# A decoder step in fp32 on one Trainium2 core: the last w_down group with tokens in PSUM's partitions, and reordered ScalarE and VectorE queues

## What is computed

```
def sq_relu_mlp(x, w_up, w_down):
    return jnp.square(jax.nn.relu(x @ w_up)) @ w_down

x = layer_norm(ALPHA * x + h, ln_g[layer, 0], ln_b[layer, 0])
x = layer_norm(ALPHA * x + sq_relu_mlp(x, w_up[layer], w_down[layer]), ln_g[layer, 1], ln_b[layer, 1])
```

## Time and profile before

| | us |
|---|---|
| median of 3 runs (lowest, highest) | 945.35 (944.09, 947.1) |
| the profiled execution, its own time | 946.36 |
| its span in the profile | 944.5 |
| PE busy | 919.8 (97%) |
| DVE busy | 629.2 (67%) |
| ACT busy | 430.9 (46%) |
| POOL busy | 56.3 (6%) |
| mean granted TensorE clock | 0.991 |

### The profile page before, as it was taken

One profiled execution on the slowest core, in us unless ns is written; L12 is line 12 of the kernel. 1 busy time (PEld: TensorE's weight loads), 2 busy tenths in 40 slices (PEclk: granted clock), 3 DMA queues, 4 the chain that ended last, 5 costly groups with the idle time before them and its releaser, 6 DMA issues.

```text
span 944.5 us, 18995 instructions
## 1 busy us (share of the span) xinstructions
PE 919.8 (97%) x7618; PEld 855.7 (91%) x7618; DVE 629.2 (67%) x1116; ACT 430.9 (46%) x801; POOL 56.3 (6%) x69
## 2 busy tenths in 40 slices
PE   9999989999999999999999999998999999999996
PEld 8999877899999999998887778877899999999994
DVE  6576568768877575676576747454468797757555
ACT  5344654356445263445344453343347644536321
POOL 0000005400000000320000000000120000000000
PEclk9999999999999999999999999999999999999997
DMA  9962213754454544566887997999855545544301
GB/s 289 279 204 90 90 45 90 214 155 139 139 169 139 173 136 143 175 211 223 290 299 241 330 368 295 392 373 340 271 175 152 160 149 185 158 134 154 115 1 56
DMA packets 134224, 182.79 MB, mean 194 GB/s; under 512 B 5845, under 2 KB 116125, under 8 KB 134136
## 3 DMA queue, kind: packets, MB, share of 16 engines
q1 hardware_dynamic: 128750, 177.29, 57.2%
q10 hardware_dynamic: 4746, 2.18, 0.9%
q0 software_dynamic: 640, 2.10, 0.8%
HBM read 175.23 MB, written 6.32 MB: 192 GB/s over the span
## 4 chain that ended last, share of the span: by engine, by line
PE 91%; DVE 4%; DMA 2%; ACT 1%; issue 1%; SPq 0%; ACTq 0%; DVEq 0%; POOL 0%; POOLq 0%
PE ps L550 24%; PE ps L552 23%; PE ps L551 23%; PE ps L887 6%; PE ps L929 3%; PE ps L985 2%; DMA page<-in_cache_v_dram 2%; PE ps L565 1%; PE ps L583 1%; PE ps L736 0%; PE ps L970 0%; PE ps L649 0%; DVE gate_o L1543 0%; DVE w_lo L1457 0%; PE ps L567 0%
## 5 line engine op out<-in xcount | busy, mean ns | idle before, releaser
L1085 ACT ACTIVATE w_hi<-raw 128x1024 fp32r<-128x1024 f32 x192 | 202.6, 1057 | 257.6 <-PE ps L552 248.4
L1457 DVE TENSOR_TENSOR w_lo<-raw,w_hi 128x1024 fp32r<-128x1024 f32 x192 | 235.1, 1225 | 113.0 <-ACT w_hi L1085 112.7
L550 PE MATMUL ps<-x_hi,w_hi 128*128 128x322 f32 (+1 forms) x888 | 279.4, 315 | 1.3 <-ACT k_turned L1355 1.3
L552 PE MATMUL ps<-x_hi,w_lo 128*128 128x322 f32 (+1 forms) x888 | 276.3, 311 | 0.0
L551 PE MATMUL ps<-x_lo,w_hi 128*128 128x322 f32 (+1 forms) x888 | 275.9, 311 | 0.0
L550 PE MATMUL ps<-h_hi,w_hi 128*128 128x320 f32 x632 | 197.4, 312 | 1.7 <-DVE h_lo L1595 1.7
L552 PE MATMUL ps<-h_hi,w_lo 128*128 128x320 f32 x632 | 195.8, 310 | 0.0
L551 PE MATMUL ps<-h_lo,w_hi 128*128 128x320 f32 x632 | 195.7, 310 | 0.0
L550 PEld LDWEIGHTS ps<-x_hi,w_hi 128*128 128x128 f32 x888 | 168.0, 189 | 6.5 <-ACT k_turned L1355 4.2
L551 PEld LDWEIGHTS ps<-x_lo,w_hi 128*128 128x128 f32 x888 | 168.5, 190 | 0.2
L552 PEld LDWEIGHTS ps<-x_hi,w_lo 128*128 128x128 f32 x888 | 167.5, 189 | 0.0
(11 more groups left out here) (349 smaller groups left out, 908.7 us busy)
## 6 DMA issues: line engine op xcount, KB each, us to landing
raw<-in_w_up_dram SPq DMA_DIRECT2D x32, 1024.0 KB, 5.7
raw<-in_w_down_dram SPq DMA_DIRECT2D x32, 1024.0 KB, 5.1
page<-in_cache_k_dram SPq DMA_DIRECT2D x64, 512.0 KB, 5.5
page<-in_cache_v_dram SPq DMA_DIRECT2D x64, 512.0 KB, 6.4
raw<-in_w_in_a_dram SPq DMA_DIRECT2D x12, 1024.0 KB, 9.2
raw<-in_w_kv_dram SPq DMA_DIRECT2D x8, 1024.0 KB, 6.8
raw<-in_w_out_a_dram SPq DMA_DIRECT2D x4, 1024.0 KB, 5.1
raw<-in_w_q_b_dram SPq DMA_DIRECT2D x4, 1024.0 KB, 5.3
```

Of the source, the lines that this page charges most:

```text
L550: mm(out, WH[t % SPL][:, k, :], hi[:, k, 0:width], start=(k == 0), stop=False)
L552: last = mm(out, WL[t % SPL][:, k, :], hi[:, k, 0:width], start=False, stop=(k == 7))
L1085: A(WH[t % SPL][:, :, :], raw[RBUF[u]][:, :, 128 * (t % 2):128 * (t % 2) + 128], ACT.Copy)\
L1457: V.tensor_tensor(WL[t % SPL][:, :, :], raw[RBUF[t // 2]][:, :, 128 * (t % 2):128 * (t % 2) + 128], WH[t % SPL][:, :, :].bitcast(F32), ALU ...
```

## The change

**The last quad.** Its 1024 rows of w_down are now loaded as rows with all 1024 columns: tile k is 128 rows (hidden columns of chunk k) by 1024. The roles are swapped: the hidden activations are stationary, 128 tokens at a time, and the weights move, 512 columns in one product, so the result has tokens in PSUM's partitions: banks 2 to 5 for two prompt tiles by two halves, banks 0 and 1 for the sample. The sample's hidden parts lie side by side in `HS` (64 columns hi, 64 lo), so that one product with `WH` makes hi in the partitions 0 to 63 and lo in 64 to 127, and one with `WL` only needs 64 columns. The stream x is added to the same banks by products of x (stationary) with the identity (`x_turn`). The last four tiles are all kept: the sample is finished first, then each prompt tile and half in turn.

**The end.** The statistics are taken from 512 columns at once (`y_stats`), each token tile is finished when its banks are complete; ACT copies the sample's lo part out of the upper partitions, DVE adds it, ACT scales the sample, POOL adds its bias, and SP stores it ahead of the prompt. The gain-and-bias pair, the sample's detour through PE and the joined statistics are gone.

**The queues.** `decay(h + 1)` is made ahead of `weights(h)`; `v_copy(7)` stands ahead of `normalised(6)`; `gated(7)` and `h_rest(7)` ahead of `state(0)`; the masked v is made by ACT (`masked`) instead of POOL; the two products of the prompt's n sum go to different columns of the array and DVE adds them; in `p_step` ACT copies what PE made ahead of the next exponent, and DVE's `head_low` stands ahead of `p_norm`.

The diff, cut to its core:

```diff
@@ -366,6 +361,17 @@
                 return ps[n % 2]
             return ps[(0, 1, 6, 7)[t % 4]]
 
+        def summed(i, half):
+
+
+            return ps[(2, 4, 0)[i] + half][:, :]
+
+        def raw_tile(t):
+            r = raw[RBUF[t // 2]]
+            if t // 8 == Q_LAST:
+                return r[:, 4 * (t % 2):4 * (t % 2) + 4, :].rearrange("p k (a n) -> p (k a) n", a=2)
+            return r[:, :, 128 * (t % 2):128 * (t % 2) + 128]
+
         def x_bank(n):
 
             return ps[(2, 3, 4, 6, 7, 1)[n % 6]]
...
@@ -424,6 +430,9 @@
                     kind, g = MLP_ORDER[q - first]
                     if kind == "u":
                         return lhs_k(w_up[m][:, 1024 * g + c:1024 * g + c + 256])
+                    if q == Q_LAST:
+                        rows = w_down[m][1024 * g + c:1024 * g + c + 256, :]
+                        return rows.rearrange("(a p) (k n) -> p a k n", p=128, k=4)
                     return lhs_k(w_down[m][1024 * g:1024 * g + 1024, c:c + 256])
             w, c0 = {Q_QK: (win, 0), Q_V: (win, 1024), Q_O: (win, 2048), Q_WOA: (w_out_a[0], 0),
                      Q_WK: (w_kv, 0), Q_WV: (w_kv, 1024), Q_WQ: (w_q_b[0], 0), Q_WOB: (w_out_b[0], 0)}[q]
...
+            sp.dma_start(y_sample.rearrange("b t c -> (b t) c"), Yt[0:64, 2, :]).then_inc(s_yp, 16)
             sp.wait_ge(s_yf, 1)
             sp.dma_start(y_prompt[0, 0:128, :], Yt[:, 0, :]).then_inc(s_yp, 16)
...
@@ -726,7 +739,7 @@
                     j = n - 2
                     pe.wait_ge(s_wk, 8)
                     pe.wait_ge(s_hg, H)
-                    pe.wait_ge(s_vm, 2 * j + 2)
+                    pe.wait_ge(s_vm, j + 1)
                     for half in range(2):
                         if j >= 2:
                             pe.wait_ge(s_cadd, 2 * j - 3 + half)
...
                         mm(o, wsK[:, q, 64 * h:64 * h + 64], VT[:, q, h, 0:128],
                            start=(q == 0), stop=(q == 1), skip_group_check=True)
-                for q in range(2):
-                    mm(ps[5][0:1, :], ones[:, 0:1], wsK[:, q, :], start=(q == 0), stop=(q == 1))
-                mm(ps[5][32:40, :], bmask[0:64, :], wsK[0:64, 2, :], start=True, stop=True).then_inc(s_np, 1)
+                mm(ps[5][0:1, :], ones[:, 0:1], wsK[:, 0, :], start=True, stop=True, skip_group_check=True)
+                mm(ps[5][64:65, :], ones[:, 0:1], wsK[:, 1, :], start=True, stop=True, skip_group_check=True)
+                mm(ps[5][32:40, :], bmask[0:64, :], wsK[0:64, 2, :], start=True, stop=True, skip_group_check=True)\
+                    .then_inc(s_np, 1)
 
             def ln_stats(l):
 
...
+            def x_turn(n):
+
+                pe.wait_ge(*emptied(8 * (Q_LAST - 1) + n))
+                c = slice(128 * (n % 4), 128 * (n % 4) + 128)
+                for i in range(3):
+                    tok = slice(128 * i, min(128 * i + 128, T))
+                    mm(summed(i, n // 4)[0:tok.stop - tok.start, c], X[:, n, tok], ident, start=False, stop=False,
+                       skip_group_check=True)
+
+            def flat(w, half):
+                return w[:, :, :].rearrange("p k n -> p (k n)")[:, 512 * half:512 * half + 512]
+
+            def down_prompt(k, i, half):
+
+                t, out, tok = 8 * Q_LAST + k, summed(i, half), slice(128 * i, 128 * i + 128)
+                wh, wl = flat(WH[t % SPL], half), flat(WL[t % SPL], half)
+                mm(out, HH[1][:, k, tok], wh, start=(k == 0), stop=False, skip_group_check=True)
+                mm(out, HH[1][:, k, tok], wl, start=False, stop=False, skip_group_check=True)
+                return mm(out, HL[1][:, k, tok], wh, start=False, stop=(k == 7), skip_group_check=True)
+
+            def down_sample(k):
+
+
+                t = 8 * Q_LAST + k
                 for half in range(2):
-                    mm(ps[4 + half][0:64, :], msT[:, :], gb2[:, 512 * half:512 * half + 512], start=False, stop=True,
-                       skip_group_check=True).then_inc(s_yz, 1)
+                    mm(summed(2, half), HS[:, k, :], flat(WH[t % SPL], half), start=(k == 0), stop=(k == 7),
+                       skip_group_check=True)
+                    last = mm(summed(2, half)[0:64, :], HS[:, k, 0:64], flat(WL[t % SPL], half), start=False,
+                              stop=(k == 7), skip_group_check=True)
+                return last
+
+            def last_down():
+                t = 8 * Q_LAST
+                pe.wait_ge(s_hl, 40 + 8 * 3 + 8)
+                pe.wait_ge(s_evr, 2)
+                for k in range(4):
+                    pe.wait_ge(s_lo, t + k + 1)
+                    for i in range(2):
+                        for half in range(2):
+                            down_prompt(k, i, half)
+                    if k == 0:
+                        pe.wait_ge(*emptied(t - 3))
+                    down_sample(k).then_inc(s_mm, 1)
+                    for n in ((), (0, 1, 2), (3, 4), (5, 6))[k]:
+                        x_turn(n)
+                for k in (4, 5, 6):
+                    pe.wait_ge(s_lo, t + k + 1)
+                    down_sample(k)
+                x_turn(7)
+                pe.wait_ge(s_lo, t + 8)
+                down_sample(7).then_inc(s_acc, 1)
+                for i in range(2):
+                    for half in range(2):
+                        for k in (4, 5, 6, 7):
+                            last = down_prompt(k, i, half)
+                        last.then_inc(s_acc, 1)
 
             def mlp(l, q0, hl0):
                 for i, (kind, g) in enumerate(MLP_ORDER):
...
@@ -1193,8 +1233,8 @@
                     normalised(h - 2)
                 if h >= 3:
                     h_rounded(h - 3)
+            v_copy(7)
             normalised(6)
-            v_copy(7)
             h_rounded(5)
             normalised(7)
             h_rounded(6)
@@ -1208,6 +1248,16 @@
             def gain_bias(l):
                 A(XH[:, :, T:TW], lnrow(lnT, l), ACT.Copy).then_inc(s_gbh, 1)
 
+            def masked(j):
+
+                if j == 0:
+                    act.wait_ge(s_hg, H)
+                    act.wait_ge(s_vc, 8)
+                for b in range(4):
+                    ins = A(Vm[:, 2 * j:2 * j + 2, b, :], VT[0:64, 2, 2 * j:2 * j + 2, 0:128], ACT.Copy,
+                            scale=bmask4[0:64, b:b + 1])
+                ins.then_inc(s_vm, 1)
+
             def x_rounded(l, n):
 
                 act.wait_ge(s_xr, 8 * l + n + 1)
...
                             if 8 * g + n >= 2:
                                 act.wait_ge(s_hl, hl0 + 8 * g + n - 1)
                             A(FS[n % 2][:, :], f[:, :], ACT.Square)
-                            A(HH[g % 2][:, n, :], f[:, :], ACT.Square).then_inc(s_hh, 1)
+                            if l == 2 and g == 3:
+                                A(HH[g % 2][:, n, 0:TP], f[:, 0:TP], ACT.Square)
+                                A(HS[:, n, 0:TS], f[:, TP:T], ACT.Square).then_inc(s_hh, 1)
+                            else:
...
@@ -1329,13 +1382,13 @@
                 A(PTt[h % 2][:, :], ps[3][:, 0:384], ACT.Copy).then_inc(s_pTc, 1)
 
             def p_step(i):
-                if 0 <= i < H:
-                    p_exp(i)
                 if 0 <= i - 2 < H:
                     act.wait_ge(s_pV, i - 2 + 1)
                     A(HH[0][:, i - 2, 0:TP], ps[0][:, 0:256], ACT.Copy).then_inc(s_xhp, 1)
                 if 0 <= i - 1 < H:
                     p_copy(i - 1)
+                if 0 <= i < H:
+                    p_exp(i)
 
             def q_lay(G):
 
...
@@ -1595,8 +1647,10 @@
                 V.tensor_tensor(HL[0][:, h, :], hg[h % 2][:, :], HH[0][:, h, :].bitcast(F32), ALU.subtract)\
                     .then_inc(s_hl, 1)
 
+            decay(0)
             for h in range(H):
-                decay(h)
+                if h + 1 < H:
+                    decay(h + 1)
                 weights(h)
                 split(8 * Q_V + h + 3)
                 if h >= 2:
@@ -1655,9 +1709,9 @@
                                                          c_bank(j, half)[:, 128 * bb:128 * bb + 128], ALU.mult, ALU.add)
                         ins.then_inc(s_cadd, 1)
 
-            state(0)
             gated(7)
             h_rest(7)
+            state(0)
             for n in range(8):
                 t = 8 * Q_WOA + n
                 residual(0, t, ALPHA)
...
@@ -1827,6 +1887,8 @@
             def p_step(i):
                 if 0 <= i < H:
                     p_max(i)
+                if i >= 2:
+                    head_low(i - 2)
                 if 0 <= i < H:
                     p_norm(i)
 
...
@@ -1988,8 +2050,6 @@
                 if i == 8:
                     reciprocals(1)
                     scale_out(1, 0)
-                if i >= 2:
-                    head_low(i - 2)
             scale_out(1, 1)
             out_low(1, 0)
             out_low(1, 1)
...
@@ -2001,25 +2061,39 @@
                 split_to(t + 3)
                 x_low(2, n)
             mlp(2, Q_MLP1, 40)
-            y_stats(7)
```

(56 more changed lines are left out.)

167 lines of the change are left out of this document (72 added, 95 removed).

## The result

| | before | changed | predicted |
|---|---|---|---|
| median, us (runs) | 944.87 (4) | 933.81 (4) | 940.1 |
| lowest, highest | 944.09, 947.1 | 933.57, 937.59 | range 932.5 to 946.5 |
| profiled execution, us | 946.36 | 933.91 | 941.1 |
| its span | 944.5 | 932.1 | |

The ratio is 0.9883, with a 95% interval of 0.9865 to 0.9902: 11.1 us faster where 5.3 were forecast. The sign and the likeliest case's mechanism for the queues were right; the size was more than twice the forecast. The time lies inside the stated range (932.5 to 946.5), but under the forecast's own (937 to 943.5) and 0.7 from rival 1's 933.1.

The account below looks back on a forecast made before the run. TensorE, busy 97% of the span, was taken as the bound, plus its waits and the end; +7.4 - 4.0 - 0.9 - 3.25 - 1.65 - 0.9 - 2.0 = -5.3 from 945.35 gave 940.1 us, range 932.5 to 946.5.

Parts of the forecast that it names:

- the likeliest case's mechanism for the queues: Reordered queues shorten TensorE's waits in four spots ahead of the final stage, bringing 8.7 us; whole forecast given 0.62.
- rival 1: Final stage: no loss at changes of stationary width, so 7.0 us go and the time is 933.1; chance 0.17.
- The step that failed: Final stage: the sample's 16 64-wide w_lo products each lose 0.27 us at the width change, 4.3 us in all.
- The price of L796: Cost of a 64-wide two-pass visit between 128-wide products, read from the old trace: 0.33 us a visit.
- the 8 identity products: Final stage: 64-wide products adding x to the sample pay the full visit cost, 2.7 us in all.
- The stage: Final eight w_down tiles: products, x additions and width changes take 41.8 us in place of 34.4, +7.4.
- The 3.6 from the last write to the end: End: time from DVE's last write to the span's end, 3.6 us with bounds 3 to 4.1, against 4.06 before.
- w_out quad: Moved v_copy and gated, v_masked off POOL: -3.25 us; clock no longer falling afterwards: -1.65.
- attention: Attention steps: h_lo ahead of p_norm and ACT's turned copy ahead of the exponent remove waits, -2.0 us (0 to -2.9).
- Rival 2: Reorderings are given back through new waits, falling clock and pages' DMA; 946.5 us, chance 0.14.
- rival 3: Slower: the sample's 16 64-wide fp32r products run in two passes, 0.94 each in place of 0.23; 951.5 us, chance 0.07.
- the rows of w_down cost 3.4: Final stage and end together: +7.4 and -4.0 leave the new w_down layout costing 3.4 us.

Follow-up runs that it names:

- wl wide: Changed kernel with the sample's w_lo products taken 128 stationary columns wide instead of 64; 934.22 us, ratio to before 0.9887.
- store last: Changed kernel with the store of y_sample put behind the three of y_prompt in SP's queue; 935.80 us, ratio to before 0.9900.
- queues only: Kernel before with all the queue reorderings and nothing else, last quad and end as before; 935.24 us, ratio to before 0.9899.

## Why the prediction was wrong in size

- **The step that failed** is "In the 16 products of 512 columns the last part should lie half hidden under a longer product: 0.27 each, 4.3 us". Measured: 0 ("wl wide"). The price of L796 was carried to products that differ from it in a single pass (and in being fp32r). The text named the counterexample (L567, single-pass and 64 wide, without loss) and gave it 0.17. The Trainium skill ("TensorEngine Tiling (Array Packing)", Key Properties) says that changing the tiling mode drains TensorE, and names no exception. If 64 stationary columns between 128 are such a change, this trace agrees for two-pass f32 products and does not for fp32r ones.
- The other half of rival 1 was wrong: the 8 identity products do pay, 2.7 us in the sum and 2.7 measured. The hit of 933.1 is in part chance.
- 0.2305 for a product of 512 columns; measured 0.234, so 29.9 for 29.5. The Trainium skill ("TensorE: Matmul & The Clock Gate", Back-to-back issue gap) gives N/2.4 + 2.5 ns for the isolated gap. By it 512 columns are 0.216, an estimate 2.3 us too little over the 128: the trace does not agree.
- The stage: +3.5 for +7.4, of which 4.3 is the failed step and 0.4 the other way the products. With the end (1.3), the queues (1.4 by the traces) and 0.5 of the rows without a term, this makes the 7.1 between the traces' 12.4 and the 5.3.
- The end: DVE's list 5.46 for 5.55 after the last product. The 3.6 from the last write to the end is the second mis-sized term, 1.1 too much: it was taken close to before's 4.06, though the sample's output had been moved ahead. With that output put last again the 3.7 is back ("store last").
- The queues: 9.1 for 8.7 ("queues only"). Decay 1.1 for 0.9; w_out quad 5.6 for 4.9 with the clock staying up; n 0.9; attention 2.6 for 2.0. The split of the w_out quad was off in its parts: `v_masked` on POOL is worth 1.6 of waits where 0.75 was taken, and `gated` ahead of `state` 0.7 of 1.14. Rival 2 falls with each experiment that undoes a part, rival 3 with the 0.234 of the 64-wide fp32r products.
- The sign of "the rows of w_down cost 3.4" was wrong, for these two terms alone: they bring 1.4.
